# Encoder layer on one core: GpSimd computes the ratio of the softmax sums and multiplies before VectorE's share is done

## The reference, cut to what matters

```python
s = jnp.einsum('bqhcd,bkhcd->bhcqk', qblk, kf) + bias[None, :, None]
pr = jax.nn.softmax(s, axis=-1)
w = pr[:, :, 0] - lam * pr[:, :, 1]
return jnp.einsum('bhqk,bkhe->bqhe', w, vf)
```

## Time and profile before

| | |
|---|---|
| median of 3 runs | 1043.45 us (1042.77 to 1043.46) |
| the profiled execution's own time | 1045.79 us |
| its span | 1044.0 us |
| attention, from its first step alone to its last turn | about 460 to 763 us of the span |

### The profile page before, as it was taken

One profiled execution on the slowest core, in us unless ns is written; L12 is line 12 of the kernel. 1 busy time (PEld: TensorE's weight loads), 2 busy tenths in 40 slices (PEclk: granted clock), 3 DMA queues, 4 the chain that ended last, 5 costly groups with the idle time before them and its releaser, 6 DMA issues.

```text
span 1044.0 us, 15464 instructions
## 1 busy us (share of the span) xinstructions
PE 1008.5 (97%) x5792; PEld 800.3 (77%) x5792; DVE 659.5 (63%) x1055; ACT 580.8 (56%) x890; POOL 500.5 (48%) x404
## 2 busy tenths in 40 slices
PE   8999999999999999989999999999999999999997
PEld 6877777767787888857777777777788888888886
DVE  4654958583493250259999999999966244445423
ACT  7738485744641131269999999999952221122112
POOL 1233245526566550036667767766667244354421
PEclk9999999999999999999999999999999999999999
DMA  9651543323255526839687478363285222432221
GB/s 337 241 169 36 172 147 101 116 81 115 77 162 164 159 81 188 243 101 243 167 197 210 110 192 223 82 159 122 68 300 167 86 87 86 137 121 86 100 87 41
DMA packets 105929, 150.34 MB, mean 144 GB/s; under 512 B 10232, under 2 KB 68728, under 8 KB 105848
## 3 DMA queue, kind: packets, MB, share of 16 engines
q1 hardware_dynamic: 105712, 149.36, 47.5%
q10 hardware_dynamic: 144, 0.00, 0.0%
HBM read 102.07 MB, written 44.11 MB: 140 GB/s over the span
## 4 chain that ended last, share of the span: by engine, by line
PE 63%; DVE 19%; issue 10%; ACT 3%; POOL 2%; DMA 2%; SPq 0%; DVEq 0%; POOLq 0%; ACTq 0%
DVE E_ L1638 11%; PE b_ps L1917 5%; PE b_ps L1919 5%; PE b_ps L1918 5%; PE b_ps L1814 4%; PE g_ps L1816 4%; PE g_ps L1814 4%; PE g_ps L1815 4%; PE b_ps L1815 4%; PE b_ps L1816 4%; PE o_ps L1980 3%; PE w_ps L1963 2%; PE h_ps L1814 2%; PE h_ps L1816 2%; PE h_ps L1815 2%
## 5 line engine op out<-in xcount | busy, mean ns | idle before, releaser
L1251 ACT ACTIVATE E_<-E_,nmax 128x1024 f32<-128x1024 f32 (+1 forms) x184 | 186.7, 1018 | 15.0 <-DVE nmax L1638 14.8
L1638 DVE CUSTOM_DVE_ANT_0 E_<-s_ps,bias 128x1024 f32<-128x1024 f32 (+1 forms) x184 | 188.0, 1056 | 3.6 <-PE s_ps L1930 3.6
L969 POOL TENSOR_TENSOR E_<-E_,ratio 128x576 f32<-128x576 f32 (+3 forms) x92 | 84.5, 919 | 85.8 <-DVE E_ L1654 85.8
L1816 PE MATMUL b_ps<-u_hi,wA_lo 128*128 128x512 f32 x288 | 113.3, 394 | 0.0
L972 POOL TENSOR_TENSOR E_<-E_ 128x576 f32<-128x576 f32 (+3 forms) x92 | 103.7, 1127 | 7.2
L1930 PE MATMUL s_ps<-KL,QL 128*128 128x512 f32 x256 | 90.7, 435 | 13.9 <-DVE nmax L1638 13.1
L1814 PE MATMUL b_ps<-u_hi,wA_hi 128*128 128x512 f32 x240 | 96.7, 403 | 5.0 <-DVE u_lo L1410 2.8
L1815 PE MATMUL b_ps<-u_lo,wA_hi 128*128 128x512 f32 x240 | 94.7, 395 | 0.0
L1963 PE MATMUL w_ps<-ident,E_ 128*128 128x128 f32 x624 | 83.4, 273 | 1.8 <-ACT WT L1282 1.7
L1282 ACT ACTIVATE WT<-w_ps 128x1024 f32<-128x1024 f32 (+1 forms) x96 | 83.3, 868 | 2.8 <-PE w_ps L1963 2.6
L1980 PE MATMUL o_ps<-WT,V 128*64 128x128 f32 x1280 | 84.0, 278 | 0.0
(11 more groups left out here) (228 smaller groups left out, 2329.6 us busy)
## 6 DMA issues: line engine op xcount, KB each, us to landing
QL<-qk_t SPq DMA_DIRECT2D x32, 256.0 KB, 6.9
KL<-qk_t SPq DMA_DIRECT2D x32, 256.0 KB, 8.2
bias<-line_d SPq DMA_DIRECT2D x8, 960.0 KB, 11.8
x_sb<-in_x SPq DMA_DIRECT2D x12, 512.0 KB, 9.0
z_ch<-z_stage SPq DMA_DIRECT2D x24, 256.0 KB, 2.7
qk_t<-qh SPq DMA_DIRECT2D x24, 256.0 KB, 2.3
qk_t<-ql SPq DMA_DIRECT2D x24, 256.0 KB, 2.8
mf<-mix_t SPq DMA_DIRECT2D x24, 256.0 KB, 3.8
```

Source lines behind the costliest of these rows:

```text
L1251: act.activation(e, e, ACT.Exp, bias=nmax[:, n % 5, c:c + 1], scale=-1.0, accum_out=sums[:, n % 5, c:c + 1]).then_inc(e_done, 1)
L1638: dve.tensor_tensor_reduce(weights_at(n)[:, c, 0:n_tok], s_ps[:, c, 0:n_tok], b[:, ::-1], -1.0, 3e38, ALU.add, ALU.min, nmax[:, n % 5, c:c ...
L1816: mm = pe.matmul(dst, sl, mh, start=False, stop=k == n - 1)
```

## The change

The ratio moves from VectorE (L1647) to a GpSimd instruction of one column. GpSimd's multiplication now waits for the ratio alone, and no longer for VectorE's combination; its addition waits for that. VectorE's combination stands between the two bias instructions of a loop step, not ahead of them. In long steps followed by long ones VectorE takes 512 columns and GpSimd 512, where it was 448 and 576.

```diff
-            return {(1, 1): 448, (1, 0): 768, (0, 0): 256, (0, 1): 128}[(int(long_now), int(long_next))]
+            return {(1, 1): 512, (1, 0): 768, (0, 0): 256, (0, 1): 128}[(int(long_now), int(long_next))]
...
+            def share(n):
+                gp.wait_ge(r_done, n + 1)
+                if n >= 4:
+                    gp.wait_ge(w_dve, n - 3)
+                    gp.wait_ge(scaled, n - 3)
+                gp.tensor_scalar(ratio[:, n % 4:n % 4 + 1], sums[:, n % 5, 0:1], rsum[:, n % 24, 1:2], neglam[:],
+                                 ALU.mult, ALU.mult).then_inc(rr_done, 1)
+
             def combine(n):
                 n_tok = UNITS[STEPS[n][2]][0]
                 one, two = (weights_at(n)[:, c, split_at(n):n_tok] for c in range(2))
-                gp.wait_ge(w_dve, n + 1)
+                gp.wait_ge(rr_done, n + 1)
                 gp.tensor_tensor(two, two, ratio[:, n % 4:n % 4 + 1].to_broadcast([P, n_tok - split_at(n)]),
                                  ALU.mult).then_inc(scaled, 1)
                 gp.wait_ge(scaled, n + 1)
+                gp.wait_ge(w_dve, n + 1)
                 gp.tensor_tensor(one, one, two, ALU.add).then_inc(w_gp, 1)
...
+                share(n)
                 combine(n)
...
                 dve.reciprocal(rsum[:, n % 24, :], sums[:, n % 5, :]).then_inc(r_done, 1)
-                dve.wait_ge(r_done, n + 1)
-                if n >= 4:
-                    dve.wait_ge(w_gp, n - 3)
-                dve.scalar_tensor_tensor(out=ratio[:, n % 4:n % 4 + 1], in0=sums[:, n % 5, 0:1],
-                                         scalar=rsum[:, n % 24, 1:2], in1=neglam[:], op0=ALU.mult, op1=ALU.mult
-                                         ).then_inc(rr_done, 1)
...
                 if n + 2 < NSTEP:
                     factor(n + 2)
+                if n + 4 < NSTEP:
+                    biased(n + 4, 0)
+                if n + 2 < NSTEP:
                     combine(n + 2)
                 if n + 4 < NSTEP:
-                    biased(n + 4, 0)
                     biased(n + 4, 1)
```

## The result

The changed kernel takes 1047.59 us (median of 7, 1046.19 to 1049.02), the kernel before 1043.45 (7 runs). The ratio is 1.0042, with a 95% interval of 1.0031 to 1.0053: it is **slower by 4.1 us**, 0.4%, clear of the noise. The forecast was 1036.2, range 1031.5 to 1046.

A forecast was written before the change was run, and what follows sets the result against it. VectorE was taken to set the pace, then the chain with GpSimd. Blocks fall from 38.0 to 37.0 and 38.3 to 37.4 us: 3.7 + 3.6 = 7.3 us off 1043.45 gives 1036.2, range 1031.5 to 1046.

The forecast's parts named there:

- What sets the pace before, and that it would pass to the chain with GpSimd: Attention's long steps: VectorE paces them at 3.47 us; afterwards mutually exclusive combination, addition and multiplication, plus ratio, at 3.32.
- A: Stretch of a 12-step block, two steps with 128 columns on VectorE, two long ones: 12.4 us, TensorE 12.29.
- The long step, 3.32 us: GpSimd chain of held-up combination, addition, ratio and multiplication with handovers: 3.32 us a step, at most 3.57.
- VectorE's own 3.16: VectorE's long step if nothing blocks: reciprocal 0.20, bias 1.14, combination 0.68, bias 1.14, together 3.16 us.
- The sum by stretches, 36.8 us, with 0.2 for coupling: Block without remainder: 13.95 + 10.49 + 12.4 = 36.8 us, plus 0.2 for unfilled gaps between stretches, 37.0.
- B: Stretch of a block with four long steps: 13.4 us by the chain, TensorE's 13.95 counts.
- C: Stretch with short bias instructions and combinations of 768 and 256 columns: VectorE 8.4 us, TensorE's 10.49 counts.
- The remainder, 0.4 us a block: Four blocks where the ratio queues behind wa_lo on GpSimd: two VectorE stalls, mostly made up, 0.4 charged, 37.4 us.
- one of my signs of being wrong: Listed sign that the forecast fails: blocks with a remainder of the output weights are longer than before.
- the rival's mechanism: GpSimd's remainder holds VectorE up for good: 3.95 us lost per such block, 1050.4 us; decides from 2.2; chance 0.18.
- Costing the ratio's departure from VectorE as a gain: 88 ratio instructions of 0.289 us leave VectorE: 25.4 us of busy time, more than can come back.
- The last steps at nothing: Last three steps: ratio through GpSimd costs two more handovers, 0.16 us, and multiplication runs earlier; nothing charged.

The follow-up runs named there:

- a4_split_576: The changed kernel with 576 columns on VectorE and 448 on GpSimd in long steps followed by long ones, for 512 and 512: 1043.75 us.
- a2_vector_ratio: The changed kernel with the ratio back on VectorE behind the reciprocal; early multiplication, new order and split of 512 stay: 1040.93 us.
- a1_ratio_ahead: The changed kernel with GpSimd's ratio for the next step ahead of the remainder of the output weights (wa_lo) in its list: 1045.16 us.
- b1_order_only: The kernel before with one edit, VectorE's combination between the two bias instructions; ratio on VectorE, late multiplication, 448 columns: 1056.87 us.
- b4_order_one_operand: The kernel before with the combination between the bias instructions and VectorE's ratio as a tensor_scalar with one streamed SBUF operand: 1040.34 us.

## Why the prediction was wrong, step by step

- **What sets the pace before, and that it would pass to the chain with GpSimd:** right, where nothing else is waited for. Combinations were held and ended 0.55 us after the multiplication (forecast 0.56), and 64 columns less for GpSimd made the kernel 3.8 us faster. But of the six long steps with a long one behind, only two of a block went from 3.47 to 3.42 us; a third went from 3.81 to 3.77, two stayed at 3.34, and the one in A that waits for scores got longer.
- **The long step, 3.32 us:** 3.42. Two terms of the sum were too small. The ratio on GpSimd takes 0.34, not 0.19, and more than the 0.277 that I gave as its bound; the handover from combination to addition takes 0.14 (632.91 to 633.05), not 0.08. With them the chain is 0.55 + 0.14 + 1.29 + 0.34 + 0.09 + 1.04 = 3.45. (GpSimd's ratio starts 0.02 us before the addition's end.) a4_split_576 bought as much back at another place of the sum. VectorE's own 3.16 was too high: the 0.20 for the reciprocal was the ratio's wait for it, and the bias instruction now starts 0.07 behind it (630.55 to 630.62). This changed nothing, as the chain is longer.
- **The sum by stretches, 36.8 us, with 0.2 for coupling:** this is the step that failed most. I took the longer of two engines in each stretch, and for B and C this was TensorE's busy time, 13.95 and 10.49, as if it could be reached. These are TensorE's score products and waits in a block without remainder (timeline of PE), cut where the earlier trace rows cuts:

```profile
690.29 0.73 PE L1936 MATMUL s_ps<-KL,QL 128*128 128x512 f32 x2
...
702.64 0.73 PE L1936 MATMUL s_ps<-KL,QL 128*128 128x512 f32 x2
...
704.77 0.73 PE L1936 MATMUL s_ps<-KL,QL 128*128 128x512 f32 x2 [0.52 <-DVE nmax L1648]
...
717.60 0.50 PE L1936 MATMUL s_ps<-Ks,Qs 128*128 128x512 f32 x1
...
728.61 0.73 PE L1936 MATMUL s_ps<-KL,QL 128*128 128x512 f32 x2
```

  A takes 12.35 us (forecast 12.4), B 14.96, C 11.01, together 38.3 where I had 37.0: 1.0 is missing in B and 0.5 in C. In B TensorE waits for VectorE's minimum (0.52 us here, and shorter waits in its weight loads), and in C its turns wait for the combination (0.61 and 0.33 us, part of the 8.6 above). VectorE comes late to B because its own four steps of A take 14.65 us (14.1 before); my 12.4 had nothing in it for its waits for scores there (timeline of DVE; the first, put down to issue, ends with the scores too):

```profile
691.16 1.23 DVE L1648 CUSTOM_DVE_ANT_0 E_<-s_ps,bias 128x1024 f32<-128x1024 f32 x1 [1.00 <-issue]
...
694.53 1.22 DVE L1648 CUSTOM_DVE_ANT_0 E_<-s_ps,bias 128x1024 f32<-128x1024 f32 x1 [0.66 <-PE s_ps L1936]
...
697.74 1.23 DVE L1648 CUSTOM_DVE_ANT_0 E_<-s_ps,bias 128x1024 f32<-128x1024 f32 x1 [0.49 <-PE s_ps L1936]
```

  Ratio and combination used to fill part of this time; the combination now stands behind the bias instruction that waits. TensorE isn't held up meanwhile: its list runs from 690.29 to 704.24 with no gap above 0.02 us. So in A VectorE waits for TensorE and in B TensorE for VectorE, and neither stretch makes up for the other. Nor is the busy time a fixed amount of work: for the same work TensorE shows 36.52 us in a block without remainder before and 37.34 now. The shortest blocks of all kernels take 37.7. Even a2_vector_ratio, with the queue and the long chain gone, has 38.0 / 37.8 against my 37.4 / 37.0: 4 x 0.6 + 3.67 x 0.8 = 5.3 us of the 11.4 by which I was off. How these 5.3 divide between the waits for minimum, combination and scores, no run separates.
- **The remainder, 0.4 us a block:** the mechanism was the one described, the size was off. The first wait was 1.33 us, the second 1.07; a block with a remainder is 0.9 longer than one without, where it was 0.3 before and 0.4 was forecast. Only the first wait lengthens the block: the second falls where VectorE would wait 1.00 us for scores anyway (the step is 3.77 us, without a remainder 3.72). That the blocks with remainder got longer than before was one of my signs of being wrong. a1_ratio_ahead took 2.4 us of it away. The queue is the rival's mechanism, at 0.9 us a block, below the 2.2 from which I let it decide alone; together with the chain and the waits between VectorE and TensorE it decided.
- **Costing the ratio's departure from VectorE as a gain:** wrong in kind. With everything else as in the change, the ratio is 6.7 us cheaper on VectorE, where it delays the next bias by 0.26 us (0.33 from the reciprocal's start in a2_vector_ratio, 0.07 in the changed kernel), than on GpSimd, where it lengthens the chain by 0.43 and queues.
- **The last steps at nothing:** no run tests it, but nothing speaks against it: from the last reciprocal to the end of the span it is 288.5 us before and 288.3 in the changed kernel.

## What to carry to other kernels

When two engines exclude each other on some instructions, count the cycle of these, with each handover, as if it were a third engine; give the cycle's longer member to the faster engine, and keep small instructions that others wait for out of it, by another form or by another engine's list. Before an instruction goes to the end of an in-order list, look at what stands ahead of it and what that waits for. Don't take the busy time of each engine in each stretch as a length that can be reached: where two engines wait for each other in turn, the block is longer than the sum of the larger ones. The length of the best stretch seen is the safer start.

## What the runs showed of the hardware

- A VectorE instruction with two streamed SBUF operands waits for a running GpSimd instruction that reads SBUF, even if it has one column; the same product with one such operand does not (0.469 and 0.273 us on the mean in the same place, b1_order_only and b4_order_one_operand). Its start-up isn't held: in a2_vector_ratio ratios that start 0.17 us before the end of an addition take 0.22, as when alone, and those that start 0.56 before it take 0.57.
- It also works the other way. In the changed kernel GpSimd's multiplication of 256 columns, 0.61 us alone, takes 1.44 when it starts 0.05 us behind a combination of 768 (timeline). The combination ends at 642.82 and the multiplication 0.47 later:

```profile
641.80 1.02 DVE L1658 SCALAR_TENSOR_TENSOR E_<-E_,ratio 128x768 f32<-128x768 f32 x1
641.85 1.44 POOL L977 TENSOR_TENSOR E_<-E_,ratio 128x256 f32<-128x256 f32 x1
```

  The Trainium skill (SBUF — State Buffer, section Who interferes with whom) calls the port pair that the two engines share an exclusive lock; for VectorE's 2-port modes it says that whoever issues first gets the shared pair for the whole instruction and the other blocks. These rows agree, for an instruction with two SBUF operands.
- GpSimd's tensor_scalar of one column takes 0.34 us with two per-partition operands, and 0.19 with two constants.
